# The second mixer's second u unit and first y unit as seven quadrant products each

## The reference, cut to what matters

```python
def rglru_mixer(xn, w_in, conv_w, conv_bias, w_rg, b_rg, w_ig, b_ig, lam, w_out):
    y_branch, u = jnp.split(xn @ w_in, 2, axis=-1)          # 512x1024 @ 1024x2048
    y_branch = jax.nn.gelu(y_branch)
    u = depthwise_conv(u, conv_w, (2, 1)) + conv_bias
    uh = u.reshape(bsz, s, N_LRU_BLOCKS, LRU_BLOCK)
    h = (rglru_direction(uh, ..., False) + rglru_direction(uh, ..., True))
    return (y_branch * h) @ w_out
# one direction:
    r = sigmoid(uh @ w_r + b_r); i = sigmoid(uh @ w_i + b_i)    # per block of 256 channels
    log_a = -RG_C * r * softplus(-lam); a = exp(log_a)
    gated = sqrt(-expm1(2 * log_a)) * (i * u)
    h = scan(h_t = a_t * h_(t-1) + gated_t), forward or backward in time
```

## Time and profile before

| what | us |
|---|---|
| median of 3 runs | 2013.72 (2012.17 to 2018.7) |
| the profiled execution, its own time | 2016.41 |
| its span | 2014.6 |
| around the span | 1.8 |
| TensorE busy | 1928.4 (96%) |
| VectorE busy | 805.2 (40%) |
| ScalarE busy | 436.1 (22%) |
| TensorE's mean granted clock | 0.985 |

### The profile page before, as it was taken

How to read it: one execution, slowest core, us unless ns; L and a number is a source line. 1 busy time by engine, 2 the same in 40 slices (tenths; PEclk the granted TensorE clock), 3 DMA queues, 4 the chain that set the end, 5 groups by cost and what they waited for, 6 DMA issues and landing times.

```text
span 2014.6 us, 21923 instructions
## 1 busy us (share of the span) xinstructions
PE 1928.4 (96%) x8574; PEld 1007.1 (50%) x8574; DVE 805.2 (40%) x2053; ACT 436.1 (22%) x887; POOL 87.2 (4%) x116
## 2 busy tenths in 40 slices
PE   7999999999999889999999999999988999999998
PEld 5886644444444335544464444444433564654555
DVE  4553454221121144455444421211114438875564
ACT  2000101111111024175210110111112532214454
POOL 0000000000000010023000000000001000000000
PEclk9999899999999899999989999999989999999999
DMA  7825389999999992121538999999999121220000
GB/s 306 198 75 227 139 329 405 429 427 429 427 427 428 424 360 84 48 84 42 230 136 350 415 429 428 427 426 429 428 424 351 65 101 42 84 84 1 11 12 22
DMA packets 46758, 512.83 MB, mean 255 GB/s; under 512 B 5296, under 2 KB 5424, under 8 KB 17328
## 3 DMA queue, kind: packets, MB, share of 16 engines
q1 hardware_dynamic: 38192, 481.38, 58.6%
q0 software_dynamic: 8448, 29.89, 3.9%
HBM read 484.90 MB, written 26.35 MB: 254 GB/s over the span
## 4 chain that ended last, share of the span: by engine, by line
PE 84%; DMA 7%; DVE 4%; ACT 2%; issue 2%; POOL 1%; SPq 0%; DVEq 0%; POOLq 0%; ACTq 0%
PE ps L1096 21%; PE ps L1135 10%; PE ps L1069 8%; PE ps L528 6%; PE ps L1941 6%; PE ps L734 5%; PE ps L1495 4%; PE ps L1658 3%; DMA ring<-in_wexp 3%; PE ps L2139 3%; PE ps L2276 3%; PE ps L1689 2%; PE ps L1160 1%; PE ps L2313 1%; DMA ring<-in_wall 1%
## 5 line engine op out<-in xcount | busy, mean ns | idle before, releaser
L1096 PE MATMUL ps<-ring,arena 128*48 128x512 f32 x1568 | 407.3, 610 | 35.9 <-issue 21.8
L1096 PEld LDWEIGHTS ps<-ring,arena 128*48 128x48 f32 x1568 | 121.2, 126 | 240.5 <-issue 239.2
L1109 DVE TENSOR_TENSOR arena<-arena,ps 48x512 f32<-48x512 f32 x64 | 44.1, 690 | 461.1 <-ACT arena L1103 461.0
L1135 PE MATMUL ps<-ring,arena 128*48 128x512 f32 x800 | 180.7, 592 | 1.1 <-DVE arena L1148 0.6
L1069 PEld LDWEIGHTS ps<-arena,h 128*128 128x128 f32 x1024 | 158.6, 190 | 44.6 <-issue 44.6
L1069 PE MATMUL ps<-arena,h 128*128 128x192 f32 (+1 forms) x1024 | 174.3, 325 | 0.0
L1096 PE MATMUL ps<-arena 128*48 128x512 f32 x480 | 159.3, 612 | 0.9 <-issue 0.9
L1103 ACT ACTIVATE arena<-ps 48x512 f32<-48x512 f32 x64 | 37.9, 592 | 475.0 <-PE ps L1096 475.0
L1941 PE MATMUL ps<-ring,arena 128*128 128x512 f32 (+3 forms) x384 | 132.7, 500 | 0.8 <-DVE arena L372 0.8
L1495 PE MATMUL ps<-ring,arena 128*128 128x512 f32 x256 | 113.0, 596 | 4.5 <-DVE arena L344 2.0
L1135 PEld LDWEIGHTS ps<-ring,arena 128*48 128x48 f32 x800 | 56.1, 123 | 115.6 <-issue 115.6
(11 more groups left out here) (305 smaller groups left out, 2303.4 us busy)
## 6 DMA issues: line engine op xcount, KB each, us to landing
ring<-in_wexp SPq DMA_DIRECT2D x148, 2048.0 KB, 19.5
arena<-in_wexp SPq DMA_DIRECT2D x44, 2048.0 KB, 20.4
ring<-in_wall SPq DMA_DIRECT2D x26, 2048.0 KB, 8.1
y_d<-arena POOLq DMA_DIRECT2D x60, 192.0 KB, 7.1
yo_d<-gbuf SPq DMA_DIRECT2D x2, 4032.0 KB, 46.3
xs_d<-h POOLq DMA_DIRECT2D x8, 512.0 KB, 5.9
ring<-in_wall SPq DMA_DIRECT2D x4, 1024.0 KB, 8.0
ring<-in_wall SPq DMA_DIRECT2D x2, 1536.0 KB, 6.3
```

What stands on the lines that cost most here:

```text
L1096: mm = pe.matmul(outs[m], xeT[:, e_ // 4 % 2, k, e_ % 4 * CAP:(e_ % 4 + 1) * CAP], ws[m][:, k, :], start=(k == 0), stop=(k == KT - 1))
L1109: dve.tensor_tensor(hh[0:CAP, e_ % 2, :], sl[0:CAP, e_ % 2, :], banks[1][64:64 + CAP, :], ALU.mult).then_inc(S["hh"], 1)
L1135: mm = pe.matmul(outs[c], hT_of(e_ % 2)[:, k, :], w[:, k, c * 512:(c + 1) * 512], start=(k == 0), stop=(k == 3))
```

## The change

Unit 1 (u) and unit 2 (y) are computed from quadrants. The weights' rows and columns are halved into A11, A12, A21, A22, the input's channels and tokens into X11, X12, X21, X22, and 7 products of 256 columns, each 2 channel groups by 4 row blocks (8 matmuls), take the place of 4 groups of 8 matmuls of 512 columns. VectorE forms four sums of the input (T1 to T4, once), four sums of weight quadrants for each unit (S1 to S4), and joins the products in 7 additions for each unit (U2, U4, 12, U3, 22, 21, 11). ScalarE copies product 1 out of its bank. Unit 1's results go to a new padded area `u4` (which is cleared first), from which VectorE convolves the last four channel blocks in the order 6, 7, 4, 5; unit 2's results go to `yT`, where gelu now works in place. TensorE's order in direction 0 is gates of blocks 0 to 3, products 1, 6, 5, 3 of unit 2, gates 4 to 7, products 7, 4, 2. Units 0 and 3 stay as they were. Two router semaphores are merged into one that counts to 2.

```diff
         def pe_mixer_b(pe):
...
             pe_project(pe, 0, 2)
-            pe_project(pe, 1)
+            pe_quads(pe, 1, (1, 6, 5, 3, 7, 4, 2))
             for d in range(2):
...
-                    pe.wait_ge(S["uct"], 2 * blk + 2)
+                    pe.wait_ge(S["uct"], 2 * blk + 2 if blk < 2 else 8)
...
-                    if c == 3:
-                        pe_project(pe, 2 + d, 0, 1)
-                pe_project(pe, 2 + d, 1)
+                    if c == 3 and d == 0:
+                        pe_quads(pe, 2, (1, 6, 5, 3))
+                    if c == 3 and d == 1:
+                        pe_project(pe, 3, 0, 1)
+                if d == 0:
+                    pe_quads(pe, 2, (7, 4, 2))
+                else:
+                    pe_project(pe, 3, 1)
+
+        def act_first_product(act, q):
+            act.wait_ge(S["b_mm"], B_AT[q][1])
+            if q == 2:
+                act.wait_ge(S["b_sum"], B_SUM[1, "11"])
+            act.activation(B_P1, b_bank(q, 1), ACT.Copy).then_inc(S["b_cp"], 1)
+        def pe_quads(pe, q, which):
+            A = {1: w[:, 0:4, LO], 2: w[:, 4:8, LO], 3: S4, 4: w[:, 4:8, HI], 5: S1, 6: S2, 7: w[:, 0:4, HI]}
+            Xq = {1: xT[:, 0:4, LO], 2: xT[:, 4:8, LO], 3: xT[:, 4:8, HI], 4: T4, 5: T1, 6: T2, 7: T3}
+            for r in which:
+                need = {6: "S2", 3: "S4", 7: "S3"}.get(r)
+                if need:
+                    pe.wait_ge(S["b_sum"], B_SUM[q, need])
...
+                for c in range(2):
+                    for k in range(4):
+                        mm = pe.matmul(b_bank(q, r)[:, c, :], A[r][:, k, c * P:(c + 1) * P], Xq[r][:, k, :], start=(k == 0), stop=(k == 3))
                 mm.then_inc(S["b_mm"], 1)
         def act_mixer_b(act):
-            for c in range(8):
+            for c in range(4):
...
+            act_first_product(act, 1)
             for d in range(2):
                 for hf in range(2):
...
+                        if d == 0 and hf == 0 and cc == 3:
+                            act.wait_ge(S["uct"], 8)
+                        if d == 0 and hf == 1 and cc == 0:
+                            act.wait_ge(S["b_mm"], B_AT[2][3])
+                        if d == 0 and hf == 1 and cc == 2:
+                            act.wait_ge(S["b_sum"], B_SUM[2, "12"])
...
+                    if d == 0 and hf == 0:
+                        act_first_product(act, 2)
...
+                if d == 0:
+                    for c in (2, 3, 0, 1):
+                        act.wait_ge(S["b_sum"], B_SUM[2, "21" if c >= 2 else "11"])
+                        act.activation(yT[:, c, :], yT[:, c, :], ACT.Gelu_apprx_tanh).then_inc(S["by"], 1)
         def dve_mixer_b(dve):
+            st.did(dve.memset(ar(20464, 4 * 516), 0.0))
+            def results(q, first):
+                if first:
+                    dve.wait_ge(S["b_cp"], q)
+                    dve.wait_ge(S["b_mm"], B_AT[q][6])
+                    total(q, "U2", B_U, B_P1, b_bank(q, 6), ALU.add)
+                    dve.wait_ge(S["b_mm"], B_AT[q][5])
+                    total(q, "U4", b_U4[q], B_U, b_bank(q, 5), ALU.add)
+                    quad(q, "12", b_U4[q], 3)
+                else:
+                    dve.wait_ge(S["b_mm"], B_AT[q][7])
+                    total(q, "U3", B_U, B_U, b_bank(q, 7), ALU.add)
+                    quad(q, "22", B_U, 5)
+                    quad(q, "21", B_U, 4)
+                    quad(q, "11", B_P1, 2)
+            rows()
+            weights(1)
+            for c in range(4):
+                convolve(c, up[:, c % 2, :])
+            results(1, True)
+            results(1, False)
+            for c in (6, 7, 4, 5):
+                convolve(c, u4[:, c - 4, :])
+            weights(2)
             for d in range(2):
                 for hf in range(2):
                     R_, I_ = bR[hf], bI[hf]
+                    if d == 0:
+                        results(2, hf == 0)
                     for cc in range(4):
```

More of the change, by code:

```diff
@@ L896, in act_router @@
         def act_router(act, l):
-            act.wait_ge(*M("r_eg", l, 1))
+            act.wait_ge(*M("r_dif", l, 1))
             act.activation(RT["eg"], RT["eg"], ACT.Exp).then_inc(S["r_exp"], 1)
-            act.wait_ge(*M("r_d2", l, 1))
+            act.wait_ge(*M("r_dif", l, 2))
             act.activation(RT["d2"], RT["d2"], ACT.Exp).then_inc(S["r_exp"], 1)
@@ L1640, in build, with b_bank @@
         scr = units["b_scratch"].ap
+        B_P1, B_U = (gbuf[:, 1, 512 * z:512 * z + 512].rearrange("p (c s) -> p c s", c=2) for z in range(2))
+        b_T = [ar(6144, 4, 256), ar(7168, 4, 256), ar(15360, 4, 256), gbuf[:, 0, :].rearrange("p (k s) -> p k s", k=4)]
+        b_S = {1: [ar(12288 + 1024 * z, 4, 256) for z in range(3)],
+               2: [scr[:, 1024 * z:1024 * z + 1024].rearrange("p (k s) -> p k s", k=4) for z in range(3)]}
+        b_U4 = {1: ar(16384, 2, 256), 2: scr[:, 3072:3584].rearrange("p (c s) -> p c s", c=2)}
+        u4 = ar(20464, 4, 516)
+        B_BANK = {1: dict(zip((1, 6, 5, 3, 7, 4, 2), (4, 5, 6, 7, 0, 1, 2))), 2: dict(zip((1, 6, 5, 3, 7, 4, 2), (3, 0, 1, 2, 3, 0, 1)))}
+        B_AT = {q: dict(zip((1, 6, 5, 3, 7, 4, 2), range(7 * q - 2, 7 * q + 5))) for q in (1, 2)}
+        B_SUM = {}
+        for q_ in (1, 2):
+            for what_ in (["T1", "T2", "T3", "T4"] if q_ == 1 else []) + ["S1", "S2", "S3", "S4", "U2", "U4", "12", "U3", "22", "21", "11"]:
+                B_SUM[q_, what_] = len(B_SUM) + 1
+        def b_bank(q, r):
+            return banks[B_BANK[q][r]][:].rearrange("p (c s) -> p c s", c=2)
         bR = [ar(16384, 4, 512), scr[:, 0:2048].rearrange("p (k s) -> p k s", k=4)]
@@ L1651, in pe_project @@
             for c4 in range(at, to):
[L1652 to L1656, removed]
-                for k in range(KT):
-                    mm = pe.matmul(banks[p_ % 4][:], w[:, k, c4 * P:(c4 + 1) * P], xT[:, k, :], start=(k == 0), stop=(k == KT - 1))
+                if q == 3:
+                    pe.wait_ge(S["b_sum"], B_SUM[2, "11"])
+                for k in range(KT):
+                    mm = pe.matmul(banks[c4][:], w[:, k, c4 * P:(c4 + 1) * P], xT[:, k, :], start=(k == 0), stop=(k == KT - 1))
+                mm.then_inc(S["b_mm"], 1)
+        def pe_quads(pe, q, which):
+            w = w8(("b", q))
+            S1, S2, S4 = b_S[q]
+            T1, T2, T3, T4 = b_T
+            A = {1: w[:, 0:4, LO], 2: w[:, 4:8, LO], 3: S4, 4: w[:, 4:8, HI], 5: S1, 6: S2, 7: w[:, 0:4, HI]}
+            Xq = {1: xT[:, 0:4, LO], 2: xT[:, 4:8, LO], 3: xT[:, 4:8, HI], 4: T4, 5: T1, 6: T2, 7: T3}
+            pe_unit(pe, ("b", q))
+            for r in which:
+                need = {6: "S2", 3: "S4", 7: "S3"}.get(r)
+                if need:
+                    pe.wait_ge(S["b_sum"], B_SUM[q, need])
+                if q == 1 and r == 7:
+                    pe.wait_ge(S["bu"], 4)
+                if q == 2 and r == 1:
+                    pe.wait_ge(S["b_sum"], B_SUM[1, "11"])
+                if q == 2 and r == 7:
+                    pe.wait_ge(S["b_cp"], 2)
+                if q == 2 and r == 4:
+                    pe.wait_ge(S["b_sum"], B_SUM[2, "U2"])
+                if q == 2 and r == 2:
+                    pe.wait_ge(S["b_sum"], B_SUM[2, "22"])
+                for c in range(2):
+                    for k in range(4):
+                        mm = pe.matmul(b_bank(q, r)[:, c, :], A[r][:, k, c * P:(c + 1) * P], Xq[r][:, k, :], start=(k == 0), stop=(k == 3))
                 mm.then_inc(S["b_mm"], 1)
@@ L1682, in pe_mixer_b @@
                     blk, m = divmod(c, 2)
-                    pe.wait_ge(S["uct"], 2 * blk + 2)
+                    pe.wait_ge(S["uct"], 2 * blk + 2 if blk < 2 else 8)
+                    if d == 0 and c == 0:
+                        pe.wait_ge(S["b_sum"], B_SUM[1, "12"])
+                        pe.wait_ge(S["b_cp"], 1)
+                    if d == 0 and c == 1:
+                        pe.wait_ge(S["b_sum"], B_SUM[1, "22"])
                     for a in range(2):
@@ L1715, in act_mixer_b @@
                         c = 4 * hf + cc
+                        if d == 0 and hf == 0 and cc == 0:
+                            act.wait_ge(S["b_sum"], B_SUM[1, "12"])
+                        if d == 0 and hf == 0 and cc == 3:
[4 more added lines that the diff above has]
+                            act.wait_ge(S["b_sum"], B_SUM[2, "12"])
                         for a, (dst, bn) in enumerate(((R_, "br"), (I_, "bi"))):
@@ L1735, in act_mixer_b @@
                         act.activation(bT[:, cc, :], bT[:, cc, :], ACT.Sqrt, scale=-1.0, bias=tiny[:, 0:1]).then_inc(S["b_sq"], 1)
[L1736 to L1739, removed]
+                if d == 0:
[3 more added lines that the diff above has]
+                else:
+                    for c4 in range(4):
+                        act.wait_ge(S["b_mm"], 18 + c4 + 1)
+                        act.activation(yT[:, 4 + c4, :], banks[c4][:], ACT.Gelu_apprx_tanh).then_inc(S["by"], 1)
         def dve_mixer_b(dve):
```

(61 more changed lines are left out.)

20 lines of the change are left out of this document (11 added, 9 removed).

## The result

The changed kernel takes 2020.2 us (median of 20 runs, 2015.6 to 2026.1), the kernel before 2016.0 in the same comparison (20 runs, 2011.5 to 2022.9). The sign is sure, the size small. The profiled execution took 2019.3 (span 2017.5).

A forecast was written before the change was run, and what follows sets the result against it. Two paths were taken to end the second mixer together: TensorE's own work and the 47 us tail behind gate group 23. Stalls less saving +0.5, clock +2.5: +3.0 on 2013.7 gives 2016.7 us, range 2009 to 2023.

The forecast's parts named there:

- the gain in whole: Second mixer: rival that neither stall comes and the saving stays, -6.6 us, 2007.1; chance 0.11 in whole or part.
- Saving: TensorE in units 1 and 2: seven products take 24.15 us instead of 27.5, 3.3 less per unit, 6.6 in all.
- Unit 1 costs nothing: VectorE's clearing, sums, convolutions and joins for unit 1 are covered by TensorE's work and add 0 us.
- S2 of unit 2 and the meetings: Before product 6: two VectorE-GpSimd meetings of 1.0 us, S2 at 871.6, needed at 872.0, no stall; bounds 0 to 1.4.
- the rival with four meetings: Before S2 of unit 2: four VectorE-GpSimd meetings start product 6 1.4 us late, +4.4, 2018.1; chance 0.08.
- First gap: TensorE before gate group 12: waits about 1.9 us for the sigmoid of group 8, delayed behind join 12.
- Second gap: TensorE before gate group 20: waits 5.3 us for the sigmoid of group 16, delayed behind join 11 and the gelus.
- The clock: TensorE behind the stalls: lower clock costs 0 after the first (other end +1.7) and +2.5 us after the second.
- the clock falls at both stalls: TensorE behind both stalls: rival that the first costs 1.7 us of clock too, +4.7, 2018.4; chance 0.12.
- Tail: Behind gate group 23: 47 us untouched, TensorE's path equally long; the rest passes the mixer's shift on one for one.
- My 0.5 us for the wait on VectorE's last product: First two output groups at the mixer's end, kernel before: 14.29 where 32 records take 13.74, some 0.5 us lost.
- Sum: Whole kernel: two stalls of 7.2 less the saving of 6.6 give +0.5, clock +2.5, together +3.0 us.

The follow-up runs named there:

- both_late: Changed kernel with unit 2's joins U2, U4, 12, 21 and 11 moved behind the squares they held up; 2007.2 us, ratio 0.9961 to the kernel before.
- unit1_only: Changed kernel with only unit 1 by 7 products, unit 2 as in the kernel before; 2013.0 us, ratio 0.9994 to the kernel before.
- second_late: Changed kernel with only unit 2's joins 21 and 11 moved behind the second half's squares and multiplies; 2009.7 us, ratio 0.9986 to the kernel before.
- first_late: Changed kernel with only unit 2's joins U2, U4, 12 moved behind the first half's squares and multiplies; 2014.3 us, ratio 1.0006 to the kernel before.
- fill: Changed kernel with unread matmuls in TensorE's gaps, 5 before gate group 12 and 12 before group 20; 2014.3 us, ratio 0.9995 to the kernel before.
- gelu_late: Changed kernel with unit 2's four gelus moved behind the first half's roots of direction 1; 2020.7 us, ratio 1.0031 to the kernel before.

## Why the prediction was right

The forecast was 2016.7, +3.0 on a median of 2013.7. It came out at 2020.2; the kernel before, timed beside it, had 2016.0, so 2.3 of the 3.5 between forecast and time are the kernel before's own scatter, and the change made +4.2 (+4.6 by the ratio), with +5.05 in the mixer. The number by itself says little: the range, 2009 to 2023, held the forecast and all rivals but the gain in whole. What bears the forecast out is that both stalls came where and as long as it said. Point by point:

- *Saving*: 3.3 per unit, shown (24.2 for seven products). both_late shows the 6.6 arriving at the end, less 0.3.
- *Unit 1 costs nothing*: held in the kernel as it is; unit1_only shows that it hangs on the four products that follow.
- *S2 of unit 2 and the meetings*: I took two meetings and S2 at 871.6, with no stall. GpSimd met VectorE three times before S2 was done (three convolution groups of 3.21), and product 6 started 0.32 late. This term was mis-sized, by one meeting: three of 0.88 make 2.6, where I had 2.0 and a margin of 0.4 left. The price of a meeting was 3.21 - 2.33 = 0.88. A fourth meeting fell on S3, which took 2.29 in place of 1.22 and which nothing waited for. So the rival with four meetings came true only at its threshold, the third, and not with its 1.4. The Trainium skill (SBUF — State Buffer, "Who interferes with whom") has the two engines exclude each other for the whole instruction. Of GpSimd's 1.28 in the meeting of 865.35, 1.08 were left when VectorE's instructions began, and VectorE lost 0.88, so the trace agrees with the rule to 0.2; on S3 1.21 were left and 1.07 lost. What my 5.0 for four full meetings overlooked is that the two don't start together: here VectorE lost no more than what was left of the other's instruction. GpSimd's operation in the third convolution, and VectorE's S3:

```profile
865.15 1.28 POOL L1950 TENSOR_TENSOR arena<-arena 128x512 f32<-128x512 f32 x1 [1.63 <-ACT arena L1788]
```

```profile
874.57 2.29 DVE L1824 TENSOR_TENSOR ring<-ring 128x1024 f32<-128x1024 f32 x1
```

- *First gap*: 1.9 said, 2.14 measured, by the chain named: join "12", squares, roots, table, sigmoid. second_late and first_late show that the place of these joins is its whole cause.
- *Second gap*: 5.3 said, 5.57 measured, by join "11", squares, roots, gelus and tables. The chain of waits of the kernel after has it in this order:

```profile
913.54 0.69 DVE arena L1824
914.22 0.61 DVE arena L1920
...
919.57 0.72 ACT arena L1806
...
922.14 1.65 ACT arena L1810 x3
...
925.93 8.58 PE ps L1738 x16
```

- *The clock*: this is the term that was mis-sized most. I took 0 at the first gap and 2.5 at the second; it was 1.77 and 1.53, together 3.3 (fill gives 3.27). That the sum came within 0.8 is luck in part: the first was too low by 1.8, the second too high by 1.0, and in first_late the second alone cost 2.67. So I was right to expect the fall after 5.6 us, and wrong to read from the earlier trace rows that a gap of 2 us is free. Of the two rows there the 8.67 was the one that applied. The windows of the earlier trace rows lie elsewhere, but the stretch of the earlier trace rows bears them out: there the clock was 0.50 from 677.7 to 684.5, from 2.1 before the restart on, which is the course that first_late took and not the one of the kernel after. The case that came true is the rival "the clock falls at both stalls", +4.7, to which I had given 0.12; it shares all its steps with the forecast but this.
- *Tail*: the chain ends as before, on group 23 and then 47 us of ScalarE, GpSimd and VectorE work, and TensorE beside it, equally late. I had said that the rest passes a shift on one for one, and that it would be wrong if the expert stage of layer 1 didn't shift with the mixer's end. In the single pair of traces it shifts by less: the mixer's end is 7.7 late, the two waits for expert weights in the chain 6.4 and 6.5 (1266.27 and 1467.95 for 1259.91 and 1461.49). That is inside the scatter named above and decides nothing. The ratios do better. In all seven kernels that were timed often, the mixer's difference lies in the interval of the ratio, and there is no sign that part of it is absorbed:

  | kernel | mixer, us | ratio as us of 2015 | its interval |
  |---|---|---|---|
  | after | +5.05 | +4.6 | +2.6 to +6.4 |
  | both_late | -6.27 | -7.9 | -10.9 to -4.8 |
  | first_late | +2.12 | +1.2 | -2.0 to +4.6 |
  | second_late | -2.20 | -2.8 | -6.0 to +0.2 |
  | fill | +1.78 | -1.0 | -5.2 to +3.0 |
  | unit1_only | -2.10 | -1.2 | -3.4 to +1.0 |
  | gelu_late | +4.88 | +6.2 | +3.6 to +8.7 |

  My 0.5 us for the wait on VectorE's last product set a length of 14.29 against a distance of starts, 13.74. Against the length 13.90 of 32 records it is 0.4; nothing hangs on it.
- *Sum*: the gaps less the saving came to +1.74 (-6.6 + 0.32 + 2.30 + 5.72) in place of +0.5: 0.3 for S2, and 0.4 for each gap, counted from start to start. The clock took 3.3 in place of 2.5. That is +5.0 for my +3.0.

## What to carry to other kernels

When work on the bounding engine becomes cheaper by moving part of it to an engine with its own ordered list, ask for each new waiting instruction in that list which ready work it now stands ahead of; here two joins held squares back by 8 and 12 us, and with the first gap's delay the second squares came 16 late. Put the waiting instruction behind the ready work, except where it frees a buffer that is wanted at once. A gap on TensorE can cost more than its length: count the granted clock behind it too, read how much from the kernel's own gaps, and take it as a range, since equal gaps cost 1.5 and 2.7 here.

## What the runs showed of the hardware

- The clock fell behind gaps of only 2.1 us: 2.14 and 2.15 before group 12 (8.80 for 7.03, in three kernels) and 2.07 before group 20 in gelu_late (8.80). It did not fall behind 0.96 in unit1_only, nor behind 2.83 in gelu_late (7.11 both), nor behind the 2.05 of the earlier trace rows. What tells these apart stays open.
- A gap of the same 5.57 us cost 1.53 in one kernel and 2.67 in the other, in one profiled execution each. The extra is close to half of the time that TensorE worked at 1.2 GHz: 2.9 and 5.2 us.
- Short matmuls with no use keep the clock up: after 24 records and an idle time of 0.30 the groups took 7.13, and the granted clock was 1.00.
- A meeting of a GpSimd operation with a convolution step cost VectorE 0.88, one with a sum of 1024 elements 1.07 (2.29 for 1.22); joins with an operand in PSUM took 0.69 whenever they ran.
